# Delta rule scalars inside the projection's pair loop, and one block of weights for w and q

## The reference, cut to what matters

```python
qkv_a = silu(causal_depthwise_conv(u @ w_in[:, :3072], conv_w))     # q, k, v; k is scaled to unit norm
beta = sigmoid(b_a)
g = -exp(a_log) * softplus(a_a + dt_bias)                           # log decay, per token and head
gc = cumsum(g within a chunk of 64)
lower = strict(k_beta @ k.T * decay);  t = lower + eye
u = solve(t, v_beta);  w = solve(t, k_beta * exp(gc))
attn = q @ k.T * decay
def step(state, ...):                                               # chunk after chunk
    v_new = u_n - w_n @ state
    out = (q_n * exp(g_n)) @ state + a_n @ v_new
    state = state * exp(g_last) + (k_n * exp(g_last - g_n)).T @ v_new
```

## Time and profile before

| | |
|---|---|
| median of three runs | 2157.24 us |
| profiled execution | 2156.17 us, span 2154.2 us, mean clock of TensorE 0.935 |
| TensorE busy (matmul) | 1859.7 us, 86% |
| VectorE busy | 1440.6 us, 67% |
| ScalarE busy | 1035.2 us, 48% |
| GpSimd busy | 370.8 us, 17% |

### The profile page before, as it was taken

How to read it: one execution, slowest core, us unless ns; L and a number is a source line. 1 busy time by engine, 2 the same in 40 slices (tenths; PEclk the granted TensorE clock), 3 DMA queues, 4 the chain that set the end, 5 groups by cost and what they waited for, 6 DMA issues and landing times. The chain is left out here.

```text
span 2154.2 us, 35801 instructions
## 1 busy us (share of the span) xinstructions
PE 1859.7 (86%) x14310; PEld 1053.4 (49%) x14310; DVE 1440.6 (67%) x1829; ACT 1035.2 (48%) x1252; POOL 370.8 (17%) x243
## 2 busy tenths in 40 slices
PE   4668987999965999995999989828999999999955
PEld 1345653434424999983444435524444454444422
DVE  3435564675755566653555658877999898888937
ACT  0425563334422222232233421117888888888934
POOL 0000000011100121120000000012445444444400
PEclk9789998999986999998999989859999999999987
DMA  8530007455335213103133312139999999999925
GB/s 334 84 94 1 1 1 283 140 181 191 124 118 126 55 49 87 47 3 98 49 98 92 132 55 85 69 148 352 398 401 416 410 402 400 400 392 388 366 111 203
DMA packets 167435, 397.73 MB, mean 185 GB/s; under 512 B 25289, under 2 KB 104450, under 8 KB 139530
## 3 DMA queue, kind: packets, MB, share of 16 engines
q1 hardware_dynamic: 149386, 353.90, 45.4%
q0 software_dynamic: 17920, 42.02, 5.0%
HBM read 361.68 MB, written 55.16 MB: 193 GB/s over the span
## 5 line engine op out<-in xcount | busy, mean ns | idle before, releaser
L2050 PE MATMUL ps<-w_gate_up_split,gathered_t 128*128 128x512 f16 x1728 | 386.9, 381 | 5.0 <-ACT gathered_t L2114 4.4
L2183 DVE SCALAR_TENSOR_TENSOR w_gate_up_split<-w_staged,w_gate_up_split 128x2048 f16<-128x2048 f32 x144 | 327.9, 2289 | 54.1 <-ACT w_gate_up_split L2105 53.2
L2105 ACT ACTIVATE w_gate_up_split<-w_staged 128x2048 f16<-128x2048 f32 x144 | 274.4, 1908 | 67.4 <-PEq L144 30.5
L1427 PE MATMUL ps<-u_transposed,w_gates_split 128*128 128x512 f16 x1152 | 253.7, 383 | 23.9 <-DVE w_gates_split L1502 20.1
L720 PE MATMUL ps<-u_transposed,w_qkv_split 128*128 128x512 f16 x1152 | 255.4, 384 | 13.9 <-DVE w_qkv_split L813 13.9
L2050 PEld LDWEIGHTS ps<-w_gate_up_split,gathered_t 128*128 128x128 f16 x1728 | 167.7, 98 | 203.4 <-ACT gathered_t L2114 6.2
L2077 PE MATMUL ps<-w_down_split,hidden_t 128*128 128x512 f16 x864 | 195.2, 383 | 7.2 <-ACT hidden_t L2151 4.2
L1427 PEld LDWEIGHTS ps<-u_transposed,w_gates_split 128*128 128x128 f16 x1152 | 113.4, 99 | 165.2 <-DVE w_gates_split L1502 20.2
L720 PEld LDWEIGHTS ps<-u_transposed,w_qkv_split 128*128 128x128 f16 x1152 | 113.0, 99 | 159.8 <-DVE w_qkv_split L813 15.1
L2183 DVE SCALAR_TENSOR_TENSOR w_down_split<-w_staged,w_down_split 128x2048 f16<-128x2048 f32 x72 | 163.8, 2288 | 16.4 <-ACT w_down_split L2105 16.2
L2105 ACT ACTIVATE w_down_split<-w_staged 128x2048 f16<-128x2048 f32 x72 | 137.1, 1907 | 42.0 <-DMA w_staged<-in_w_down 20.4
(11 more groups left out here) (352 smaller groups left out, 2879.1 us busy)
## 6 DMA issues: line engine op xcount, KB each, us to landing
w_staged<-in_w_gate SPq DMA_DIRECT2D x72, 1024.0 KB, 11.2
w_staged<-in_w_up SPq DMA_DIRECT2D x72, 1024.0 KB
w_staged<-in_w_down SPq DMA_DIRECT2D x72, 1024.0 KB
w_ada_ring<-in_w_ada SPq DMA_DIRECT2D x8, 2048.0 KB
w_qkv_ring<-in_w_in SPq DMA_DIRECT2D x12, 1024.0 KB, 5.8
qkv_scratch<-qkv_silu POOLq DMA_DIRECT2D x24, 512.0 KB, 3.0
qkv_tile<-qkv_scratch SPq DMA_DIRECT2D x8, 1536.0 KB, 9.3
w_gates_ring<-in_w_in SPq DMA_DIRECT2D x24, 512.0 KB, 5.2
```

Source lines behind the costliest of these rows:

```text
L1427: last = pe.matmul(ps[:, 2 * j + half, :], w16[:, side, j, wp, k, :], m.u[:, up, k, half * 512:half * 512 + 512], start=(t == 0), stop=(t ...
L2050: last = pe.matmul(ps[:, GU[s] + j, :], xt[:, s, xp, k, :], w16[:, j, wp, k, :], start=(k == 0 and t == 0), stop=(k == KC - 1 and t == 2))
L2105: nc.scalar.activation(split(kind, 0, int(q)), staged(m, kind, int(q)), ACT.Identity, scale=W_SCALE).then_inc(hi_ok[kind + q], 1)
L2183: nc.vector.scalar_tensor_tensor(split(kind, 1, int(q)), staged(m, kind, int(q)), W_SCALE, split(kind, 0, int(q)), ALU.mult, ALU.subtract) ...
```

## The change

Three edits in one.

1. The prologue of `delta_rule` moves into `project`; ScalarE loads another table of functions eight times for it, at pairs 5 (two), 6 (two, one of them ahead of SiLU), 7, 10 (two) and 11. ScalarE does the sigmoid and the exponential of `a_log` behind pair 5, the softplus exponential behind pair 6, the exponentials of the decays and the square root behind pair 10. VectorE does the arguments behind pair 5, the log decays behind pair 7, their sums behind pair 9, the key scalars ahead of pair 11's convolution. TensorE makes the decay sums behind pair 9's products and two transposes behind pair 10's. GpSimd fetches the square sums at pair 9 and stores the decay rows at pair 11. `delta_rule` begins with the loads of the decay rows, then queries and keys in one load and values in another. The squares of the keys are written to a part of `m.yb`, after it is stored.
2. Modulation pieces 4 and 5 are loaded earlier; piece 7 has a bias buffer and a PSUM bank of its own, is loaded right behind piece 6, and both are summed over the partitions behind the products of pair 11. Its sum on VectorE stands behind pair 10's convolution.
3. In the chunk steps, `w` (transposed) and the scaled queries stand side by side in a tile `wq`, 64 columns each, and one matmul per head reads the state for both. The output is then made as rows of tokens: `write_state` adds `at` times `v_new` for each half, ScalarE copies the rows (`output_rows`), TensorE turns them (`turn_output`) and ScalarE copies the result (`output`). The key rows are turned behind level 5, and `decayed_keys` stands behind `scale_inverse`.

```diff
-    ADA_AT = {p: n for n, p in enumerate((0, 1, 2, 3, 8, 9, 10, 11))}
+    ADA_AT = {0: (0,), 1: (1,), 2: (2,), 3: (3,), 8: (4,), 9: (5,), 10: (6, 7)}
...
-                    sp.wait_ge(ada_out[n % 2], 16 * (n // 2))
+                    if n < LATE - 1:
+                        sp.wait_ge(ada_out[n % 2], 16 * (n // 2))
...
-                n = {4: 2, 5: 3, 6: None, 9: 4, 10: 5, 11: 6}.get(p)
+                n = {4: 2, 5: 3, 6: 4, 7: 5, 11: 6}.get(p)
...
+                    if n == LATE - 1:
+                        pe.wait_ge(exp_ok, 1)
...
+                if p == 8:
+                    pe.wait_ge(g_ok, 1)
+                    for n, lhs in enumerate((m.const("cum"), m.const("chunk_ones"), m.const("half")[:, 0:P], m.const("half")[:, P:])):
+                        last = pe.matmul(ps[:, 7, n * 64:(n + 1) * 64], lhs, tab[:, :, G, :], start=True, stop=True)
+                    last.then_inc(sums_mm, 1)
+                if p == 9:
+                    pe.wait_ge(tab_ok, 1)
+                    pe.transpose(ps[0:TC * H, 5, 0:P], sc[:, 3].rearrange("p c h -> p (c h)"), m.const("ident")).then_inc(gc_t, 1)
+                    pe.wait_ge(ssq_in, 16)
+                    pe.transpose(ps[:, 6, 0:TC * H], ssq_rows[:], m.const("ident")[0:TC * H, 0:TC * H]).then_inc(ssq_t, 1)
...
+                if p == 5:
+                    nc.scalar.activation(tab[:, :, BETA, :], m.ba[:, :, 0:H], ACT.Sigmoid).then_inc(beta_ok, 1)
+                    nc.scalar.activation(ea[:], m.small[:, 0:H], ACT.Exp).then_inc(ea_ok, 1)
+                if p == 6:
+                    act.wait_ge(xa, 2)
+                    nc.scalar.activation(sc[:, 2], sc[:, 1], ACT.Exp, scale=-1.0).then_inc(y_ok, 1)
+                if p == 10:
+                    act.wait_ge(gc_t, 1)
+                    nc.scalar.activation(gc_rows[:, 1, :], ps[0:TC * H, 5, 0:P], ACT.Exp)
+                    nc.scalar.activation(gc_rows[:, 0, :], ps[0:TC * H, 5, 0:P], ACT.Identity).then_inc(gc_row_ok, 1)
+                    nc.scalar.activation(sc[:, 6], tab[:, :, GC, :], ACT.Exp)
+                    nc.scalar.activation(tab[:, :, EKD, :], sc[:, 7], ACT.Exp)
+                    nc.scalar.activation(egl[:].rearrange("p s c h -> p (s c h)"), ps[:, 7, 128:256], ACT.Exp).then_inc(exp_ok, 1)
+                    act.wait_ge(ssq_t, 1)
+                    act.wait_ge(eps_ok, 1)
+                    nc.scalar.activation(inv[:, 0], ps[:, 6, 0:TC * H].rearrange("p (h c) -> p c h", h=H), ACT.Sqrt, bias=eps[:, 0:1]).then_inc(root_ok, 1)
...
+                if p == 11:
+                    key_scalars()
                 convolve(p)
-                if p - 1 in ADA_AT:
-                    row(ADA_AT[p - 1])
-            row(LATE - 1)
+                if p == 10:
+                    partial(LATE - 1)
+                for n in ADA_AT.get(p - 1, ()):
+                    row(n)
+                if p == 5:
+                    nc.vector.memset(eps[:], NORM_EPS).then_inc(eps_ok, 1)
+                    softplus_arguments()
+                if p == 7:
+                    log_decays()
+                if p == 9:
+                    decay_sums()
...
+                sp.dma_start(tiles[:, c % 2, 0:2 * H], qkv[:, 0:2 * H, c * P:(c + 1) * P]).then_inc(qkv_in[c % 2], 16)
+                sp.dma_start(tiles[:, c % 2, 2 * H:], qkv[:, 2 * H:, c * P:(c + 1) * P]).then_inc(v_in[c % 2], 16)
...
-            sp.dma_start(ssq[:], m.ssq_dram.rearrange("h (c p) -> (h c) p", p=P)).then_inc(S("ssq_in"), 16)
+            load_decays(0)
             load_qkv(0)
+            load_decays(1)
             load_qkv(1)
-            sp.wait_ge(S("gc_row_ok"), 2)
-            sp.dma_start(m.gc_dram, gc_rows[:]).then_inc(S("gc_out"), 16)
-            sp.wait_ge(S("gc_out"), 16)
-            load_decays(0)
-            load_decays(1)
...
-                    last = pe.matmul(ps[r, 4 + h // 4, wide4(h)], wt[:, s, h, :], s_[:, h, :], start=True, stop=True)
+                    last = pe.matmul(ps[:, 4 + 2 * s + h // 4, wide4(h)], wq[:, s, h, :], s_[:, h, :], start=(h % 4 == 0), stop=False,
...
-                for h in range(H):
-                    pe.matmul(ps[:, 6 + s, at8(h)], s_[:, h, :], qg[:, h, r], start=(h == 0), stop=False, skip_group_check=True)
...
+                    if s == 1:
+                        pe.wait_ge(S("o_row_ok"), c * 2 + 1)
...
+                        last = pe.matmul(ps[:, 6 - 2 * s + h // 4, wide4(h)], kd[r, h, :], vn[r, h, :], start=True, stop=True)
                     last.then_inc(S("dstate_mm"), 1)
-                if s == 1:
-                    for h in range(H):
-                        for half, q in enumerate(rows):
-                            last = pe.matmul(ps[:, 6 + half, at8(h)], vn[q, h, :], at[q, c % 2, h, :], start=False, stop=True, skip_group_check=True)
-                    last.then_inc(S("o_mm"), 1)
+                for h in range(H):
+                    last = pe.matmul(ps[rows[1 - s], 4 + 2 * s + h // 4, wide4(h)], at[r, c % 2, h, :], vn[r, h, :], start=False, stop=True,
+                                     skip_group_check=True)
+                last.then_inc(S("o_mm"), 1)
...
-                token_rows(c)
+                if c >= 1:
+                    turn_output(c - 1)
+                value_rows(c)
                 level(c, 5)
+                key_rows(c)
...
+            turn_output(LAST)
...
+            def output_rows(c, s):
+                r = rows[1 - s]
+                act.wait_ge(S("o_mm"), c * 2 + s + 1)
+                nc.scalar.activation(orow[r].rearrange("p (b h) t -> p b (h t)", b=2), ps[r, 4 + 2 * s:6 + 2 * s, :], ACT.Identity
+                                     ).then_inc(S("o_row_ok"), 1)
...
-                    output(c - 1)
+                    if c >= 1 and k % 2 == 0:
+                        output_rows(c - 1, k // 2 - 1)
                 if c < LAST:
                     decays(c + 1)
                 level(c, 5)
+                if c >= 1:
+                    output(c - 1)
                 token_rows(c)
...
                 level(c, 4)
-                decayed_keys(c)
                 level(c, 5)
                 scale_inverse(c)
+                decayed_keys(c)
```

More of the change, by code:

```diff
@@ L780, in silus @@
                     act.wait_ge(silu_ok, p * 2 + 2)
[L781 removed]
+                    if p == KEYED[0]:
+                        act.wait_ge(yb_out, 16)
+                    else:
                         act.wait_ge(ssq_mm, p - KEYED[0])
[L783 removed]
+                    nc.scalar.activation(sq, silu[:, p % 2], ACT.Square).then_inc(sq_ok, 1)
             def sums(p):
@@ new lines, in decay_sums, with key_scalars @@
+            def decay_sums():
+                dve.wait_ge(sums_mm, 1)
+                sums = ps[:, 7, 0:128].rearrange("p (n c h) -> p n c h", n=2, c=TC)
+                step(nc.vector.tensor_copy(tab[:, :, GC, :], sums[:, 0]))
+                step(nc.vector.tensor_copy(sc[:, 3], sums[:, 0]))
+                step.settle()
+                nc.vector.tensor_tensor(sc[:, 7], sums[:, 1], tab[:, :, GC, :], ALU.subtract).then_inc(tab_ok, 1)
+            def key_scalars():
+                dve.wait_ge(root_ok, 1)
+                step(nc.vector.reciprocal(inv[:, 0], inv[:, 0]))
+                step.settle()
+                dve.wait_ge(beta_ok, 1)
+                step(nc.vector.tensor_tensor(tab[:, :, BETA, :], tab[:, :, BETA, :], inv[:, 0], ALU.mult))
+                step.settle()
+                step(nc.vector.tensor_tensor(inv[:, 1], tab[:, :, BETA, :], inv[:, 0], ALU.mult))
+                step.settle()
+                dve.wait_ge(exp_ok, 1)
+                step(nc.vector.tensor_tensor(tab[:, :, BG, :], inv[:, 1], sc[:, 6], ALU.mult))
+                step(nc.vector.tensor_scalar(tab[:, :, NBETA, :], inv[:, 1], -1.0, None, ALU.mult))
+                step.settle()
@@ L882, in _ @@
                         pool.dma_start(m.ssq_dram[n:n + 1, :], ssq[:]).then_inc(ssq_out[b], 16)
+                if p == 9:
+                    for b in range(2):
+                        pool.wait_ge(ssq_out[b], 64)
+                    pool.dma_start(ssq_rows[:], m.ssq_dram.rearrange("h (c p) -> (h c) p", p=P)).then_inc(ssq_in, 16)
+                if p == 11:
+                    pool.wait_ge(gc_row_ok, 1)
+                    pool.dma_start(m.gc_dram, gc_rows[:]).then_inc(gc_out, 16)
                 for b in range(2):
@@ L913, in delta_rule @@
         vt, kt, kd, u, vn = wide("v_rows"), wide("k_rows"), wide("k_decayed"), wide("u_rows"), wide("v_new")
[L914 to L923, removed]
+        s_, sg, orow = wide("state"), wide("state_decayed"), wide("output_rows")
+        wq = m.sb("w_and_q", [P, 2, H, P], ctx=ctx)
+        tab, egl = m.tab, m.egl
         G, GC, NBETA, EKD, BG, BETA = range(6)
         sems = {n: m.sem("delta_" + n) for n in (
-            "ssq_in ssq_t root_ok xa beta_ok ea_ok y_ok g_ok sums_mm exp_ok tab_ok gc_t gc_row_ok gc_out x_ok ds_ok dt_ok scaled_ok kk_mm qk_mm "
```

(15 more changed lines are left out.)

178 lines of the change are left out of this document (79 added, 99 removed).

## The result

The changed kernel takes 2134.11 us (median of 2128.28 to 2138.39), the kernel before 2156.65; ratio 0.9898, 95% interval 0.9879 to 0.9916. Forecast: 2130, 2122 to 2138. From profiled span to profiled span it is 2154.2 to 2132.6, -21.6, against -27 forecast.

| stretch | before | after | moved | forecast |
|---|---|---|---|---|
| to the block of `delta_rule` | 651.32 | 641.19 | -10.1 | -11 |
| block to first inversion | 26.75 | 17.07 | -9.7 | -10.7 |
| first inversion to second chunk | 19.81 | 22.26 | +2.4 | -0.5 |
| six chunks | 38.03 each | 36.21 each | -10.9 | -4.8 |
| last chunk, to its u product | 38.71 | 36.26 | -2.5 | 0 |

A forecast was written before the change was run, and what follows sets the result against it. TensorE bounds the pair loop and steady chunks, nothing the gaps between. End of `project` -11, start of `delta_rule` -10.7 and chunks -5.3 make -27: 2156.17 to 2129.2, median 1.1 above, so 2130 us; 8-in-10 range 2122 to 2138.

The forecast's parts named there:

- the two large terms: End of `project`, -11 us, and start of `delta_rule`, -10.7 us, out of -27 in all.
- End of project: Piece 7 loaded behind piece 6, last convolution and last DMA issue earlier: -11 us, between -5 and -13.
- the 601: End of `project`: the forecast is wrong if pair 10's sums start after 601 us.
- loads that advance side by side: Rival: pieces 6 and 7 share bandwidth, piece 6 lands up to 6 us later; 2136 us, chance 0.10.
- Start of `delta_rule`: From its block to the first inversion, 16.0 us instead of 26.75: -10.7 us, between -7.5 and -15.
- Steady chunk: TensorE's order in each chunk step of `delta_rule`: -0.8 us a chunk, bounds -3 and +2.9.
- The failing term: Chunk steps: output product of eight 64-row matmuls with 128 columns, not run in pairs, 1.95 us.
- The read: Chunk steps: wide state read for w and q together, 1.93 us for x16, floor 1.87, ceiling 3.80.
- level 5 to the next chunk: Chunk steps: next chunk starts 3.8 us after level 5 begins, instead of 2.9.
- The last gains nothing: Last chunk: no gain, its tail having the keys' copy, another output product, a row copy and a turn in line.
- Chunk 0: First chunk of `delta_rule`: a gain of 0.5 us.
- Hidden work: Pair loop of `project`: added table loads (1.28 us each) and small operations cost nothing, beyond 1.3 us of TensorE.

The follow-up runs named there:

- the second base: The changed kernel run again unedited, on the chip of the trial with 7 added products: 2134.04 us, ratio 0.9899 to the kernel before.

## Why the prediction was right or wrong

The direction was right, and so were the two large terms. That the total came within 4.1 us of the forecast is partly luck: the seven chunk steps gained 8.6 us more than forecast, and chunk 0 and the last stretch lost 10.1 us that I had not counted.

- End of project: -10.1 for -11. Right; undoing it gave 11 to 12 back. The sums of pair 10 began at 601.68, past the 601 that I had named as a sign of being wrong. The rival behind that sign, loads that advance side by side, is still out: the load was issued 0.96 later (593.71 for 592.75) and took no longer (7.97 for 8.12).
- Start of `delta_rule`: -9.7 for -10.7. The data came 11.3 us after the block, not 10; from data to inversion 5.8, not 6.0. No run undoes this move alone; its worth is read from the profiles.
- Steady chunk: -1.8, not -0.8. The failing term is the output product, "which all use one quarter of the array and so cannot run in pairs: 8 x 2 records x 0.12 = 1.95". Among themselves they did not (16 records took 1.89 us with the output product first), but the last of them run beside the next level's. Against the earlier trace rows both writes with their output products cost 1.1 us more a chunk, not 2.15. The read (1.95 for 1.93) and level 5 to the next chunk (3.64 for 3.8) held.
- "The last gains nothing": up to its u product it gained 2.5, and the last stretch lost 7.2. I named the added work there without a price (it is 1.6 us), and did not think of what the emptier order does to the clock. The separate query products had filled waits.
- Chunk 0: +2.4, not -0.5: the stop, then half clock. In the second base, with a shorter stop (1.76 us) and full clock behind it, it was +0.2.
- Hidden work: right. TensorE has no idle time from 480 to 558.5 us, and table loads cost 1.28 each and no more.

## What to carry to other kernels

Work that is removed may have been the cover of a wait: price what TensorE's clock does in the emptier stretch, above all at a block's end. A few unneeded products in such waits kept the clock up in all three trials that filled every wait, and a fall costs 5.5 to 7.8 us here. Judge such a trial by the stretch that it changes, since other blocks move the whole by as much from run to run. Small products in different quarters of the array overlap with their neighbours, as they did here, so count a block by the start of the next, not by its own records.

## What the runs showed of the hardware

- In the same program TensorE's granted clock sometimes falls to 1.2 GHz behind waits of 0.95 and 1.22 us and sometimes doesn't: 20.91, 26.48 and 28.68 us for one stretch.
- While bulk loads were under way TensorE stopped for 0.6 to 2.7 us in the middle of a group, waiting for nothing that the profile shows: at one fixed record in eight of eight profiles. With the loads held it did not stop there, in one of two it stopped 0.99 us in the next chunk, and with the old chunk code there was no stop.
- Two 2 MB loads issued 0.92 us apart on one queue did not advance side by side: the first's data was taken up after 7.97 us, against 8.12 for a lone one.
- Behind the last output copy, where all the kernels have the same code, the profiles took 1168.3 to 1175.1 us.
